# Two-layer encoder trunk: running sums as one-pass products with high and low parts, value projection 512 columns wide

## The reference, cut to what matters

```
z = einsum('bhqd,bhkd->bhqk', q, k) * 64**-0.5
strict = s_pos < t_pos
log_keep = where(strict, log_sigmoid(-z), 0)
later = cumsum(log_keep, axis=3, reverse=True) - log_keep
att = where(strict, exp(log_sigmoid(z) + later), 0)
out = einsum('bhqk,bhkd->bhqd', att, v) @ w_o
```

## Time and profile before

| | us |
|---|---|
| median of 3 runs | 1178.18 |
| lowest and highest run | 1172.83, 1178.29 |
| profiled execution | 1177.06 |
| its span, first to last instruction | 1175.2 |
| TensorE busy | 1125.4 (96%) |
| VectorE busy | 748.8 (64%) |
| ScalarE busy | 569.7 (48%) |
| GpSimd busy | 287.6 (24%) |

### The profile page before, as it was taken

How to read it: one execution, slowest core, us unless ns; L and a number is a source line. 1 busy time by engine, 2 the same in 40 slices (tenths; PEclk the granted TensorE clock), 3 DMA queues, 4 the chain that set the end, 5 groups by cost and what they waited for, 6 DMA issues and landing times.

```text
span 1175.2 us, 22820 instructions
## 1 busy us (share of the span) xinstructions
PE 1125.4 (96%) x9077; PEld 1103.8 (94%) x9077; DVE 748.8 (64%) x848; ACT 569.7 (48%) x780; POOL 287.6 (24%) x294
## 2 busy tenths in 40 slices
PE   6899999888889999999999999999999999999997
PEld 6899999888889999999999999999988899999997
DVE  6778866779666655555785555566433565555576
ACT  6644444354576444444564444445555544444453
POOL 7799998923111100000120000001000110000011
PEclk9999999999799999999999999999999999999999
DMA  8466653341136665665455566565422366566542
GB/s 214 147 181 186 182 165 118 99 126 37 36 96 201 178 180 179 186 183 183 155 174 176 184 189 179 180 188 164 131 91 90 112 181 183 179 184 185 184 144 90
DMA packets 156294, 182.78 MB, mean 156 GB/s; under 512 B 16072, under 2 KB 143696, under 8 KB 156240
## 3 DMA queue, kind: packets, MB, share of 16 engines
q1 hardware_dynamic: 156096, 181.99, 51.7%
q10 hardware_dynamic: 144, 0.04, 0.0%
HBM read 180.95 MB, written 1.05 MB: 155 GB/s over the span
## 4 chain that ended last, share of the span: by engine, by line
PE 67%; DVE 7%; ACT 3%; issue 2%; POOL 1%; POOLq 0%; DVEq 0%; ACTq 0%
PE bank L1321 14%; PE bank L1323 13%; PE bank L1322 13%; PE acc L1321 6%; PE acc L1323 6%; PE acc L1322 6%; DVE w_lo L914 2%; DVE op_lo L927 2%; ACT w_hi L622 1%; PE acc L1527 1%; PE acc L1446 1%; PE acc L1540 1%; ACT op_hi L634 1%; PE acc L1516 1%; PE bank L1565 1%
## 5 line engine op out<-in xcount | busy, mean ns | idle before, releaser
L914 DVE TENSOR_TENSOR w_lo<-raw,w_hi 128x1024 fp32r<-128x1024 f32 x340 | 448.3, 1322 | 311.5 <-ACT w_hi L622 310.0
L622 ACT ACTIVATE w_hi<-raw 128x1024 fp32r<-128x1024 f32 x340 | 359.3, 1059 | 455.7 <-PE bank L1323 284.2
L1321 PE MATMUL bank<-op_hi,w_hi 128*128 128x256 f32 x1728 | 498.1, 288 | 14.7 <-DVE op_lo L927 6.0
L1322 PE MATMUL bank<-op_hi,w_lo 128*128 128x256 f32 x1728 | 492.1, 285 | 0.0
L1323 PE MATMUL bank<-op_lo,w_hi 128*128 128x256 f32 x1728 | 492.0, 285 | 0.0
L1321 PEld LDWEIGHTS bank<-op_hi,w_hi 128*128 128x128 f32 x1728 | 334.6, 194 | 19.5 <-issue 11.7
L1322 PEld LDWEIGHTS bank<-op_hi,w_lo 128*128 128x128 f32 x1728 | 334.7, 194 | 0.0
L1323 PEld LDWEIGHTS bank<-op_lo,w_hi 128*128 128x128 f32 x1728 | 334.6, 194 | 0.0
L1321 PE MATMUL acc<-g_hi,w_hi 128*128 128x256 f32 x704 | 199.3, 283 | 0.0
L1322 PE MATMUL acc<-g_hi,w_lo 128*128 128x256 f32 x704 | 198.9, 282 | 0.0
L1323 PE MATMUL acc<-g_lo,w_hi 128*128 128x256 f32 x704 | 198.8, 282 | 0.0
(11 more groups left out here) (261 smaller groups left out, 1315.0 us busy)
## 6 DMA issues: line engine op xcount, KB each, us to landing
raw<-in_ffn_w_dram SPq DMA_DIRECT2D x264, 512.0 KB, 3.7
raw<-in_sb_w_qkv_dram SPq DMA_DIRECT2D x24, 512.0 KB, 3.5
raw<-in_s_w_glu_dram SPq DMA_DIRECT2D x16, 512.0 KB, 3.5
raw<-in_ple_gate_dram SPq DMA_DIRECT2D x16, 512.0 KB, 3.6
raw<-in_s_w_in_dram SPq DMA_DIRECT2D x8, 512.0 KB, 3.6
raw<-in_sb_w_o_dram SPq DMA_DIRECT2D x8, 512.0 KB, 3.5
raw<-in_ple_proj_dram SPq DMA_DIRECT2D x4, 512.0 KB, 3.4
rows_in<-in_x_dram SPq DMA_DIRECT2D x2, 512.0 KB, 4.4
```

Source lines behind the costliest of these rows:

```text
L622: act.activation(w_hi[:, slot, :], raw[:, slot, :], ACT.Copy).then_inc(hi_done, 1)
L914: dve.tensor_tensor(w_lo[:, slot, :], raw[:, slot, :], w_hi[:, slot, :].bitcast(F32), ALU.subtract)\
L1321: pe.matmul(o, wh, xh, start=start, stop=False, skip_group_check=True)
L1322: pe.matmul(o, wl, xh, start=False, stop=False, skip_group_check=True)
```

## The change

The drops are split into a high and a low part, `drop_both`: ScalarE copies head s-1's masked drops to fp32r in step s (after the log of head s, before the exponential of head s-2), and VectorE subtracts (after the drops of head s). TensorE waits for that subtraction instead of for the masks. The triangle and the ones become fp32r, and for each part there is one product of 384 columns with the triangle and one of 128 columns with the ones, in place of three f32 products.

In the value projection a chunk has 256 rows x 512 columns. Four chunks make a half (512 of the 1024 columns), whose two frame blocks lie in two banks of their own; a matmul moves 512 columns, and a chunk has 2 k x 2 frame blocks x 3 = 12 of them. The waits on `bank_taken` within the projection go, since the second half uses other banks (`acc[2]`, `acc[3]`), and ScalarE copies 128x512 at a time.

```
+        drop_both = sb("drop_both", [P, DEPTH, 2, HW], F32R, at=...)
+        val_bank = [[... for t in pair] for pair in ((bank[0], bank[1]), (acc[2], acc[3]))]
...
@@ SP: load_attn @@
-                for j in range(NB):
-                    load_group(st.n0 + 2 * j, w, 2 * D + 256 * j)
+                for i in range(8):
+                    n, half, kk = st.n0 + i, i // 4, i % 4
+                    src = w[256 * kk:256 * kk + 256, 2 * D + 512 * half:2 * D + 512 * half + 512]
+                    load(n, n % RING, src.rearrange("(k p) c -> p k c", p=P), True)
...
@@ ScalarE: attention @@
-                for j in range(NB):
-                    split(n0 + 4 + 2 * j)
+                for half in range(2):
+                    for n in range(4 + 4 * half, 7 + 4 * half):
+                        split(n0 + n)
                     act.wait_ge(r_ready, st.v + 1)
-                    act.wait_ge(pe_done, n0 + 2 * j + 2)
+                    act.wait_ge(pe_done, n0 + 4 * half + 4)
                     for tb in range(TB):
-                        act.activation(val[:, tb, 256 * j:256 * j + 256], bank[j % 2][:, tb, :], ACT.Copy,
-                                       scale=r_col[:, tb:tb + 1]).then_inc(bank_taken, 1)
-                    split(n0 + 5 + 2 * j)
+                        act.activation(val[:, tb, 512 * half:512 * half + 512], val_bank[half][tb], ACT.Copy,
+                                       scale=r_col[:, tb:tb + 1]).then_inc(bank_taken, 2)
+                    split(n0 + 7 + 4 * half)
...
+                    h = s - 1
+                    if 0 <= h < NH:
+                        act.wait_ge(drop_masked, 2 * h + 2)
+                        if h >= DEPTH:
+                            act.wait_ge(exponent_done, h - DEPTH + 1)
+                        act.activation(drop_both[:, h % DEPTH, 0], drop[:, h % DEPTH], ACT.Copy).then_inc(drop_hi_done, 1)
...
@@ VectorE: attention @@
+                    h = s - 1
+                    if 0 <= h < NH:
+                        dve.wait_ge(drop_hi_done, h + 1)
+                        dve.tensor_tensor(drop_both[:, h % DEPTH, 1], drop[:, h % DEPTH],
+                                          drop_both[:, h % DEPTH, 0].bitcast(F32), ALU.subtract).then_inc(drop_lo_done, 1)
...
@@ TensorE: head_step @@
-                    pe.wait_ge(drop_masked, 2 * h + 2)
-                    d = drop[:, h % DEPTH]
+                    pe.wait_ge(drop_lo_done, h + 1)
...
-                    add(zb[:, 0:T], minus_tri[:, :], d[:, 0:T])
-                    add(zb[:, P:T], minus_ones[:, :], d[:, T:HW])
-                    add(zb[:, T:HW], minus_tri[:, :], d[:, T:HW])
+                    for i in range(2):
+                        d = drop_both[:, h % DEPTH, i]
+                        add(zb[:, 0:HW], minus_tri[:, :], d)
+                        add(zb[:, P:T], minus_ones[:, :], d[:, T:HW])
...
@@ TensorE: attention, the value projection @@
+                for i in range(8):
+                    n, half = n0 + i, i // 4
+                    pe.wait_ge(lo_done, n + 1)
+                    for kk in range(2):
+                        k = 2 * (i % 4) + kk
+                        if half == 0:
+                            pe.wait_ge(op_lo_done, KD * u + k + 1)
+                        wh, wl = (w[:, n % RING, kk * 512:(kk + 1) * 512] for w in (w_hi, w_lo))
+                        for tb in range(TB):
+                            xh, xl = (o[:, HALF[u], k, tb * P:(tb + 1) * P] for o in (op_hi, op_lo))
+                            o = val_bank[half][tb]
+                            pe.matmul(o, xh, wh, start=k == 0, stop=False)
+                            pe.matmul(o, xh, wl, start=False, stop=False)
+                            mm = pe.matmul(o, xl, wh, start=False, stop=k == KD - 1)
+                        if kk == 1:
+                            mm.then_inc(pe_done, 1)
+                        if i == 2 and kk == 0:
+                            stat_sum(st.v)
+                        if i == 3 and kk == 1:
+                            stat_spread(st.v)
+                pe.wait_ge(bank_taken, 4)
```

More of the change, by code:

```diff
@@ L130, in hybrid_trunk @@
         p_lo = sb("p_lo", [P, 2, T], F32R)
-        minus_tri = sb("minus_tri", [P, P])
-        minus_ones = sb("minus_ones", [P, P])
+        minus_tri = sb("minus_tri", [P, P], F32R)
+        minus_ones = sb("minus_ones", [P, P], F32R)
         ident_b = sb("ident_b", [P, P], BF16)
@@ L167, in hybrid_trunk @@
                                            for i, name in enumerate(("z_abs", "z_exp", "z_log", "drop", "att")))
+        drop_both = sb("drop_both", [P, DEPTH, 2, HW], F32R, at=mixer + 12 * KD * T + 20 * DEPTH * HW)
         assert top[0] <= nc.sbuf_usable_end
@@ L210, in hybrid_trunk @@
         drop_done, drop_masked = sem("drop_done"), sem("drop_masked")
+        drop_hi_done, drop_lo_done = sem("drop_hi_done"), sem("drop_lo_done")
         exponent_done, att_done, o_done = sem("exponent_done"), sem("att_done"), sem("o_done")
@@ L305, in hybrid_trunk @@
         ple_bank = [bank[0], bank[1], misc.rearrange("p (k t) -> p k t", k=2), bank[1]]
+        val_bank = [[t.rearrange("p a t -> p (a t)") for t in pair] for pair in ((bank[0], bank[1]), (acc[2], acc[3]))]
         z_bank = [acc[0].rearrange("p a t -> p (a t)"), acc[1].rearrange("p a t -> p (a t)"), misc]
@@ L321, in load @@
                 if shape_k:
-                    dst = dst.rearrange("p (k c) -> p k c", k=4)
+                    dst = dst.rearrange("p (k c) -> p k c", k=src.shape[1])
                 sp.dma_start(dst, src).then_inc(raw_landed[slot], 16)
@@ L445, in _ @@
             pool.wait_ge(consts_ready, 5)
-            pool.memset(minus_tri[:, :], -1.0).then_inc(masks_made, 1)
-            pool.memset(minus_ones[:, :], -1.0).then_inc(masks_made, 1)
+            pool.memset(minus_tri[:, :].bitcast(F32), -1.0).then_inc(masks_made, 1)
+            pool.memset(minus_ones[:, :].bitcast(F32), -1.0).then_inc(masks_made, 1)
             pool.memset(ident_b[:, :], 0.0).then_inc(masks_made, 1)
@@ L450, in _ @@
             pool.wait_ge(masks_made, 4)
-            pool.affine_select(out=minus_tri[:, :], in_=minus_tri[:, :], compare_op=ALU.is_ge, fill=0.0, base=0,
+            pool.affine_select(out=minus_tri[:, :], in_=minus_tri[:, :].bitcast(F32), compare_op=ALU.is_ge, fill=0.0, base=0,
                                pattern=[[-1, P]], channel_multiplier=1).then_inc(masks_made, 1)
@@ L1549, in attention @@
                 o_set[0] = u + 1
[L1551 to L1574, removed]
@@ L1575, in attention @@
-                pe.wait_ge(bank_taken, 6)
+                for i in range(8):
[18 more added lines that the diff above has]
+                            stat_spread(st.v)
@@ L1576, in attention @@
+                pe.wait_ge(bank_taken, 4)
                 group(n0 + 8, bank[0], u)
-                pe.wait_ge(bank_taken, 8)
                 group(n0 + 10, bank[1], u)
```

## The result

The changed kernel takes 1168.78 us (median of 7 runs, 1166.15 to 1172.41), the one before 1177.23 (7 runs, 1172.83 to 1178.91). The ratio is 0.9934 with a 95% interval of 0.9912 to 0.9957, which is 7.8 us less (5.1 to 10.4). The forecast for a median was 1171.6.

The account below looks back on a forecast made before the run. TensorE's own instruction stream was taken to set the pace of layer 1's attention. 1177.06 less 5.6 (running sums) and 1.0 (value projection) is 1170.5, plus 1.1 for a median 1171.6; range 1165.5 to 1178.

Parts of the forecast that it names:

- Running sums, 0.35 us per head: Head step on TensorE: the running-sum block takes 0.63 us against 0.98, 0.35 less.
- The columns' count with 0.013 on top: One-pass products on TensorE: cost is columns at 2.4 GHz plus 0.013 us, 0.173 for 384 columns, 0.227 for 512.
- the best case: Running sums: only 0.003 on top of the columns, 0.59 us per head, 6.2 us less in all.
- Rival B: Head steps: narrow one-pass products cost as much as f32 ones; heads give 1.3 us, total 1175.9; chance 0.18.
- 16 heads, 5.6 us: Head loop: all 16 heads are in steps that TensorE sets, so the running sums save 5.6 us.
- the last split being late: Loop's last weight split on VectorE: 1.1 us of cover shrinks to a tie; cost 0, up to 0.3 us.
- Value projection, 1.0 us: Value projection: 72 products of 512 columns at 0.227 us against 0.240 for two of 256, 1.0 us less.
- The gap of 2.5 us in one piece: Value projection: TensorE idles 2.5 us in one piece, 799.6 to 802.1, awaiting the third chunk's low part.
- Rival A: Value projection: the idle gap brings TensorE's clock to half for 3.4 us, costing 1.7 us, total 1173.3; chance 0.31.
- Cover in full steps, 2.0 us: Head loop: w_lo ends at 871.9, its chunk starts at 873.9; 2.0 us of cover remain, so no cost.
- The new product's own cover: Head loop: drop_lo is ready about 2.9 us after the step's scores, its products come 5.4 after; no cost.
- Sum: Whole kernel: 1177.06 - 5.6 - 1.0 = 1170.5, plus 1.1 for a median gives 1171.6; 6.6 us below.

Follow-up runs that it names:

- the kernel with both moved: Changed kernel with the third chunk's low part earlier on VectorE, and drop_both's copy and subtraction at their step's start; ratio 0.9919 to the kernel before.
- a_both: The changed kernel again, unaltered, as yardstick of the first group of follow-up runs; ratio 0.9922 to the kernel before.
- b_load: Changed kernel with one more 128x384 copy on ScalarE and two more subtractions on VectorE per head step, results unused; ratio 0.9969 to the kernel before.

## Why the prediction was right, step by step

- **Running sums, 0.35 us per head.** Right: 0.63 for 0.98. The terms are not all right: the first wide product costs 0.28 with the open load (0.10 + 0.173 was the sum). The middle narrow product and the wide one behind it were put at 0.115 and 0.173 and cost 0.06 and 0.22. The sum is the same; that the wide product pays for its weights in place of the narrow one is a reading of these starts and not tested. The 0.115 rested on a misread row: 1.89/16 holds the last record's way through the pipe, and the starts in it are 0.112 apart. The columns' count with 0.013 on top held for 512 columns (0.227). For 384 it fits if the open load is 0.10 as estimated. For 128 the starts were 0.06 apart, where it gives 0.067. No run shows the 0.003 on top of the columns that the best case used. Rival B (narrow products cost as f32 ones, 0.22) is refuted.
- **16 heads, 5.6 us.** It was 5.3. From the step up to head 15's scores on, 0.36 us are lost. I had put up to 0.3 on the last split being late. That split ends at 914.92 and its chunk starts at 915.06, so the 1.1 us of cover of the earlier trace rows are indeed used up, but 0.21 of the loss lies elsewhere. Rows of the changed kernel in step 15:

```profile
906.08 0.51 ACT L872 ACTIVATE drop_both<-drop 128x384 fp32r<-128x384 f32 x1
...
906.49 0.47 ACT L878 ACTIVATE att<-acc 128x384 f32<-128x384 f32 x1
...
906.86 0.38 ACT L882 ACTIVATE op_hi<-acc 128x256 fp32r<-128x256 f32 x1
...
907.27 0.42 DVE L1284 TENSOR_TENSOR op_lo<-acc,op_hi 128x256 fp32r<-128x256 f32 x1
...
907.74 0.38 PE L1340 MATMUL bank<-op_hi,w_hi 128*128 128x256 f32 x1
```

The high copy (906.08) stands ahead of the exponential and of the output's high part on ScalarE, so the output's low part ends at 907.69, and TensorE starts at 907.74, 0.21 us later than in the kernel with both moved. The prediction named the output's high and low part as queued behind the copy and then followed only w_lo. That kernel has 5.54 in this step.
- **Value projection, 1.0 us.** It was 0.85, with the clock up. The pace is 0.227 in most places; just behind the gap single starts are 0.231 to 0.240 apart, in a_both too.
- **The gap of 2.5 us in one piece.** Right: 2.2 to 2.3 us of wait in every profile with the wide projection, the old VectorE order and nothing added to the gap. Rival A (the gap brings the clock down), which had 0.31, came true in one profile of five (798.0 in the first one); it then cost 1.5 us (41.44 against 39.98) where 1.7 were put. The six gaps of before that it was weighed by are 1.9 to 2.3 us long between matmul records, not 2.0 to 2.6. The rule of the Trainium skill (TensorE: Matmul & The Clock Gate, Why this matters for your kernels) would have cleared the gap; by that one profile it does not hold here as a safe bound, and with a gap of 3.4 us the fall came as it says.
- **Cover in full steps, 2.0 us.** 2.2 by the rows, and b_load's added work costs nothing there. The agreement is luck, as two terms were off and cancel. The split's low part ends 5.8 us after the step's scores (866.55) where it was 5.5: 0.3 later, not 0.5 to 0.8. And its chunk starts 8.0 us after them (868.75) where it was 8.7: 0.7 earlier and not 0.35, because two blocks of running sums lie in between. The new product's own cover was misread too: the low part of the drops is ready 3.6 us after the scores (864.35), not 2.9, since it stands behind the drops of the next head on VectorE, and its product comes 6.4 after them (867.12), not 5.4. Neither made a wait.
- **Sum.** 6.6 was forecast in all, 7.8 came (5.1 to 10.4), and 6.1 is what the changed stage shows, so the mechanism is right and the rest of the total is luck of the clock or unexplained: in the profiled execution 1.5 us were lost to rival A, and 5.7 were gained ahead of and behind the two parts with changed code. Over all runs, 41 of before and 19 of the changed kernel, the means are 1176.9 and 1169.2, 7.8 us apart with 1.2 of uncertainty; with each run's mean clock taken into account by a straight line (34 runs of before have it on record), 7.1 apart with 0.7. So 1 to 1.7 us are not explained by the stage. A part may be that the clock's fall near the end (1129.8 to 1141.1), which cost 1.73 us in all three profiles of before, came in six of eleven changed ones only, and cost 1.45 there. Whether the change has a part in that, or these were chance, stays open.

## What to carry to other kernels

Where the list of waits shows an engine waiting for nothing but itself over a whole stage, starts of neighbours times their number give a change's worth to a few tenths of a us; here two independent edits came out at 5.3 for 5.6 and 0.85 for 1.0. When work is put into the middle of another engine's step, follow each thing queued behind it, not only the longest, into the shortest step of the loop. Before a wait of TensorE on VectorE is taken as given, see whether the instructions in it are as long as the same ones elsewhere: here the four that made the gap took 4.22 us beside GpSimd, where two took 0.87 alone. And judge a change of half a per cent by its own stage in the profile: the medians differ by 8.45 us, and the changed stage accounts for 6.1 of them.

## What the runs showed of the hardware

- A one-pass fp32r product at clock 1.00 costs its columns at 2.4 GHz plus about 13 ns: 0.120 (256 columns), about 0.17 (384, an estimate: 0.28 less the open load of 0.10), 0.227 (512). Widening from 256 to 512 gains 5% of the stream.
- A one-pass product of 128 columns was followed after 0.06 us by one with new weights, and the wide one behind it took 0.22 for 0.17. Records of f32 products start 0.112 apart with 64 columns and 0.109 to 0.112 with 128: half the columns gained nothing.
- TensorE's clock: idle pieces of 2.2 to 2.3 us were followed by 0.50 in one profile of five, one of 3.4 us was (one profile), and with small products in it the clock stayed at 1.00 and 1.57 us were saved (one profile). Three gaps that all kernels share, of 2.1, 2.1 and 3.1 us, had a fall around their end in four, nine and eleven of fourteen profiles.
- VectorE's subtraction of 1024 columns takes 1.88 us beside GpSimd's additions and 1.2 alone; its low part of 256 activation columns takes up to 1.52 beside them and 0.48 alone.
